# Memory attention in two token blocks, with the expert gathers of the first block beside the attention of the second

## The reference

```python
def memory_cross_attention(h, mem_n, wq, wkv, wo):      # 4 heads of 256
    q = (h @ wq).reshape(B_, S, N_XATTN_HEADS, XATTN_HEAD_DIM)
    ...
    p = jax.nn.softmax(jnp.einsum('bshd,bmhd->bhsm', q, k) * (XATTN_HEAD_DIM ** -0.5), axis=-1)
    o = jnp.einsum('bhsm,bmhd->bshd', p, v).reshape(B_, S, N_XATTN_HEADS * XATTN_HEAD_DIM)
    return o @ wo

def peer_ffn(h, wq, subkeys, u, v):                     # 8 heads, 128 x 128 experts
    q = (xt @ wq).reshape(T, PEER_HEADS, 2, PEER_HALF)
    s = jnp.einsum('thpc,hpnc->thpn', q, subkeys)
    s_top, i_top = lax.top_k(s, PEER_TOPK)              # 16 of each half
    cand = s_top[:, :, 0, :, None] + s_top[:, :, 1, None, :]
    best, pos = lax.top_k(cand.reshape(T, PEER_HEADS, 256), PEER_TOPK)
    gates = jax.nn.softmax(best, axis=-1)
    ...
    def block(args):                                    # 128 tokens at a time
        act = jax.nn.gelu(jnp.einsum('cd,ced->ce', xb, u[eb])) * gb
        return jnp.einsum('ce,ced->cd', act, v[eb])

x = x + memory_cross_attention(rms_norm(x, xattn_norm_g), rms_norm(mem, mem_norm_g), ...)
x = x + peer_ffn(rms_norm(x, ffn_norm_g), ...)
```

## Time and profile before

| what | value |
|---|---|
| median of 3 runs | 1732.67 us (1731.45 to 1732.8) |
| profiled execution | 1734.02 us, of it 1732.2 us from first to last instruction |
| mean granted clock of TensorE | 0.973 |
| busy | PE 1570.4 us (91%), DVE 1214.4 (70%), ACT 851.1 (49%), POOL 357.7 (21%) |
| 256 gathers | 312.52 to 947.35 us (issue), 268.45 MB on their queue |
| attention, from the end of `wq` to the first gather | 245 to 312.5 us |

### The profile page before, as it was taken

The page is one execution under the profiler, slowest core; times in us unless marked ns, Lnnn a source line. Parts: engine busy times, 40 slices in busy tenths (PEclk is TensorE's granted clock), DMA queues, the critical chain, the costliest instruction groups (busy, mean ns, idle before and its releaser), DMA issues.

```text
span 1732.2 us, 23839 instructions
## 1 busy us (share of the span) xinstructions
PE 1570.4 (91%) x9202; PEld 1192.7 (69%) x9202; DVE 1214.4 (70%) x2403; ACT 851.1 (49%) x1713; POOL 357.7 (21%) x326
## 2 busy tenths in 40 slices
PE   6999988789997787878888999999999999999999
PEld 5899988555542232322242688989999977789999
DVE  5797665777888888845654689666776548777764
ACT  5657734444454444433433663245554436465542
POOL 1010102344454444444433003100000200010000
PEclk9999999899999999999999999999999999899999
DMA  7333443799999999999999432024444522035544
GB/s 270 123 122 122 152 165 120 318 403 425 415 425 426 427 427 427 427 427 427 428 427 427 161 135 98 26 98 146 174 182 152 200 98 98 25 122 191 176 167 149
DMA packets 63592, 421.13 MB, mean 243 GB/s; under 512 B 8180, under 2 KB 11512, under 8 KB 15608
## 3 DMA queue, kind: packets, MB, share of 16 engines
q0 software_dynamic: 36864, 268.45, 36.9%
q1 hardware_dynamic: 23952, 148.70, 24.0%
q10 hardware_dynamic: 2664, 2.47, 0.4%
HBM read 418.54 MB, written 1.05 MB: 242 GB/s over the span
## 4 chain that ended last, share of the span: by engine, by line
PE 63%; DMA 19%; DVE 11%; ACT 5%; issue 2%; SPq 0%; ACTq 0%; DVEq 0%
PE bank L377 62%; DMA uv<-in_uv,idx 18%; DVE lows L440 3%; DVE uv L1418 2%; ACT dg L389 2%; PE bank L382 1%; DMA slabs<-in_w_in 1%; ACT wp L385 1%; ACT acts L389 1%; ACT L389 0%; DVE cacc L393 0%; ACT wf L385 0%; DVE rsb L543 0%; DVE t L722 0%; DMA slabs<-in_sk 0%
## 5 line engine op out<-in xcount | busy, mean ns | idle before, releaser
L377 PE MATMUL bank<-uv,dg 128*128 128x512 f32 x1024 | 494.6, 619 | 83.7 <-ACT dg L389 83.4
L377 PEld LDWEIGHTS bank<-uv,dg 128*128 128x128 f32 x1024 | 183.2, 193 | 373.4 <-ACT dg L389 215.3
L1418 DVE CUSTOM_DVE_ANT_0 uv<-uv,htok 128x1024 f32<-128x1024 f32 x256 | 313.0, 1223 | 163.6 <-DMA uv<-in_uv,idx 160.5
L1532 POOL DMA_INDIRECT uv<-in_uv,idx x256 | 281.4, 1099 | 372.7 <-PE bank L377 324.1
L377 PE MATMUL bank<-hn,lows 128*128 128x272 f32 (+2 forms) x704 | 200.9, 285 | 0.0
L440 DVE TENSOR_TENSOR lows<-slabs,wp 128x2048 fp32r<-128x2048 f32 (+1 forms) x78 | 167.7, 2150 | 45.9 <-ACT wp L385 45.7
L389 ACT ACTIVATE acts<-acts 128x1 f32<-128x1 f32 x256 | 51.4, 201 | 279.3 <-DVE acts L1418 278.7
L385 ACT ACTIVATE wp<-slabs 128x2048 fp32r<-128x2048 f32 (+1 forms) x78 | 140.7, 1804 | 86.1 <-DMA slabs<-in_dn 29.7
L557 POOL TENSOR_TENSOR sqT<-sqT 128x256 f32<-128x256 f32 (+1 forms) x42 | 44.4, 1058 | 623.6 <-ACT sqT L389 621.4
L440 DVE TENSOR_TENSOR lows<-slabs,whl 128x2048 fp32r<-128x2048 f32 (+1 forms) x52 | 108.2, 2081 | 36.8 <-ACT whl L385 36.7
L377 PE MATMUL bank<-hh,lows 128*128 128x272 f32 x448 | 133.1, 297 | 0.0
(11 more groups left out here) (380 smaller groups left out, 3005.0 us busy)
## 6 DMA issues: line engine op xcount, KB each, us to landing
slabs<-in_up SPq DMA_DIRECT2D x44, 1024.0 KB, 4.8
slabs<-in_w_in SPq DMA_DIRECT2D x28, 1024.0 KB, 4.8
slabs<-in_dn SPq DMA_DIRECT2D x32, 704.0 KB, 4.1
slabs<-in_wkv SPq DMA_DIRECT2D x8, 1024.0 KB, 4.8
slabs<-in_w_out SPq DMA_DIRECT2D x8, 1024.0 KB, 4.8
slabs<-in_pq SPq DMA_DIRECT2D x8, 1024.0 KB, 4.9
slabs<-in_wq SPq DMA_DIRECT2D x4, 1024.0 KB, 4.8
slabs<-in_wo SPq DMA_DIRECT2D x4, 1024.0 KB, 4.8
```

Of the source, the lines that this page charges most:

```text
L377: ins = T.e.matmul(pr[2] if len(pr) > 2 else out, pr[0], pr[1], start=(start and k == 0), stop=(stop and k == len(pairs) - 1), skip_group_ ...
L1418: V.e.tensor_tensor_reduce(u_, u_, htok[:, n, :], 1.0, 0.0, ALU.mult, ALU.add, acts[:, n, e_:e_ + 1]).then_inc(*V.up("dot", q))
L1532: G.e.indirect_dma_start(uv[q % NU][:, :], None, d["uv"][:, :], bass.IndirectOffsetOnAxis(ap=idx[:, n, e_:e_ + 1], axis=0)).then_inc(s_uv[ ...
```

## The change

The stage `xat` is gone. Its work, the end of the mixer's projection, the choice for head 0 and the gathers and accumulations up to gather 116 of the first block follow one list written out by hand (`XAT_ORDER`) that all engines walk, each taking its own tokens. Behind it the planner goes on with 2 steps for each gather.

- The attention goes by units (head, block), the first block ahead of the second. `pT` holds 128 tokens.
- The output projection is token-major: for one block, one slab and one head 6 matmuls with 256 columns (`wo.n.i.h`: block n, slab i, head h). They accumulate in banks 4 + 2n and 5 + 2n upon the residual, which is brought there by products with the identity (`xx`). The expert sums accumulate upon that in the same banks, and the final copy adds nothing.
- Of each block the gain is applied on VectorE in token-major layout (`xg`), the squares are summed by ScalarE from the bank (`sq2`), and the tokens are transposed (`ht`) and split (`hh`, `hl`). The root of the norm (`rcol`) is applied in the scores' copy and in the Gelu's scale.
- Head 0's query goes block by block (`q0`, `qe`, `qx`, `qy`, scores `s0`, their copy `sy`). Its slab (`pq.0`) has a place of its own and is loaded ahead of `wo`, as are the gains in rows (0.5 MB).
- The buffers of the gathers lie over tiles of the attention. `row_buffer_free` says what each waits for: 4, 2, 0, 1 and 3 need parts of the attention or the first block's projection, and 5, 6 and 7 need the whole output projection of the second block.

```diff
+XAT_ORDER = """
...
+xa.2.0.10 wo.0.1.1 wo.0.2.1 xa.3.0.7 xa.3.0.8 xa.1.1.1 wo.0.2.2 wo.0.1.2 lo.wo.3 xa.0.1.5 wo.0.0.1 wo.0.0.2 xa.3.0.9 xa.3.0.10
...
+wo.1.3.1 wo.1.2.3 u.4 wo.1.0.0 wo.1.0.1 wo.1.1.1 wo.1.0.2 wo.1.1.2 u.2 wo.1.0.3 wo.1.1.3 u.0 xg.1.0 u.1 wo.1.3.2
...
+            elif what == "wo":
+                _, n, i, h = x
+                k = PLACE["wo", i]
+                w = weights(k)
+                split_tensor(k)
+                T.wait_ge(*V.at("xl", h, n))
+                o = B[4 + 2 * n + i // 2][:, (i % 2) * 256:(i % 2) * 256 + 256]
+                ins = mm(o, [(O[n][q][:, c, :], w[p][:, c, :]) for c in (2 * h, 2 * h + 1) for p, q in TERMS], False, False)
...
+            elif what == "xg":
+                _, n, half = x
+                V.wait_ge(s_row, 16)
+                for i in (2 * half, 2 * half + 1):
+                    for h in range(4):
+                        V.wait_ge(*T.at("wo", n, i, h))
...
+        def row_buffer_free(q):
+
+            units = [(h, n) for h in range(4) for n in range(2)]
+            if q == 0:
+                for h in range(4):
+                    G.wait_ge(*T.at("xO", h, 0))
+            elif q in (1, 2):
+                for u in units:
+                    G.wait_ge(*T.at("xS", *u))
+            elif q == 4:
+                for u in units:
+                    G.wait_ge(*T.at("xO", *u))
+            else:
+                for i in range(4):
+                    for h in range(4):
+                        G.wait_ge(*T.at("wo", 0 if q == 3 else 1, i, h))
...
-            for q in range(2 * P + LAG):
+            begin = max(x[1] for x in done if x[0] == "u") + 1
+            for q in range(begin, 2 * P + LAG):
                 if q < 2 * P:
                     n, e_ = divmod(q, P)
                     while ("choose", n, e_ // 16, 18) not in taken:
                         pump(1, q)
                     out.append(("u", q))
-                    pump(3 if q < 16 else 2, q)
+                    pump(3 if q < 80 else 2, q)
```

More of the change, by code:

```diff
@@ L252, in build @@
         zero = top.enter_context(ExitStack())
+        with ExitStack() as ph:
+            gains = [sbuf(ph, f"row{q}", [P, NC, T1]) for q in range(2)]
         MM = [sbuf(zero, f"mm{q}", [P, NC, T1], F32R) for q in range(2)]
+        with ExitStack() as ph:
+            pq0 = sbuf(ph, "pq0", [P, 2, SLOTW], F32R)
         sc = sbuf(zero, "sc", [P, 2, 16, P])
@@ L276, in build @@
             qT = sbuf(ph, "qT", [P, 8, T1])
[L277 to L280, removed]
+            O = [[sbuf(ph, f"o0{q}", [P, NC, P], F32R) for q in range(2)]]
+            eb = [sbuf(ph, f"eb{i}", [P, T1]) for i in range(4)]
+            pT = [sbuf(ph, f"pT{i}", [P, 2, P]) for i in range(4)]
         mid.close()
@@ L288, in build @@
             oneh = sbuf(ph, "oneh", [P, 256])
-            uv = [sbuf(ph, f"uv{i}", [P, 2 * D]) for i in range(NU)]
+            with ExitStack() as two:
+                O.append([sbuf(two, f"o1{q}", [P, NC, P], F32R) for q in range(2)])
+            for i in (5, 2, 4, 1, 3, 0):
+                uv[i] = sbuf(ph, f"uv{i}", [P, 2 * D])
             dg = [sbuf(ph, f"dg{i}", [P, P]) for i in range(NDG)]
@@ L1264, in scores_of @@
             return [("spj", h, 0, 0), ("spj", h, 0, 1), ("sev", h, 0), ("spj", h, 1, 0), ("spj", h, 1, 1), ("sev", h, 1), ("ssc", h), ("scp", h)]
-        def spread(steps, more):
-            out = list(steps)
-            for k, x in enumerate(more):
-                out.insert(2 * k + 1, x)
-            return out
         def choice_of(n, h):
@@ L1276, in peer_plan @@
         def peer_plan():
-            first, second = scores_of(0), choice_of(0, 0)
-            out = first + second[:7] + [("tokens",)] + second[7:11] + [("gexp", 0, 0)] + second[11:] + scores_of(1)
-            todo = []
-            for h in range(1, 7):
-                steps = choice_of(0, h)
-                todo += [("parts", h + 1)] + spread(steps, scores_of(h + 1))
-            todo += choice_of(0, 7)
+            out, todo = [], []
+            for h in range(1, 8):
+                todo += [("parts", h)] + scores_of(h) + choice_of(0, h)
             for h in range(8):
                 todo += choice_of(1, h)
-            taken, late = {("choose", 0, 0, 18)}, []
+            done = set(XAT)
+            todo = [x for x in todo if x not in done and not (x[0] == "parts" and ("hi", "pq", x[1]) in done)]
+            taken, late = {x for x in done if x[0] == "choose" and x[3] == 18}, []
             def pump(steps, q):
@@ L1314, in build, with scores_at @@
         PEER = peer_plan()
+        def scores_at(n, h, q):
+            return sc[:, n, 2 * h + q, :] if h else sc0[:, n, q, :]
         def cand_jobs(n, h):
-            return [(sv_[:, q, :], si[:, q, :], sc[:, n, 2 * h + q, :], s2[:, q, 0:P]) for q in range(2)]
+            return [(sv_[:, q, :], si[:, q, :], scores_at(n, h, q), s2[:, q, 0:P]) for q in range(2)]
         def final_jobs():
```

761 lines of the change are left out of this document (457 added, 304 removed).

## The result

The changed kernel takes 1743.45 us (median of 7, 1737.67 to 1750.04) against 1732.8 us (median of 7, 1731.29 to 1734.88): ratio 1.0062, 95% interval 1.0048 to 1.0076. It is 10.7 us slower. I had forecast 1730; the time lies in the stated range and on the other side of no change. Its single times spread by 12 us, those of the kernel before by 4.

The account below looks back on a forecast made before the run. The gathers' transfers were taken to bound the stretch from 312.5 to 960, TensorE the rest. Head start -26.6, slabs +9.8, late indices +11.7, late buffers +2.3 sum to -2.8 us: about 1730, range 1721 to 1744.

Parts of the forecast that it names:

- Head start: Before the gathers' stream: the first gather goes at 285.9, 26.6 us earlier, with VectorE setting the start.
- the hole behind the first five: After five gathers, three wait for buffers to about 302; slabs ready by then fill the gap, charged nothing.
- Slabs: In the gathers' stream: four more slabs of 1 MB move beside gathers, adding 9.8 us.
- Late indices: At first gathers of heads 1, 3, 4 and the second block: holes for want of indices, together +11.7 us.
- L: Time of a gather from issue to landing, taken as 7.0 us between bounds 5.3 and 8.6.
- Late buffers: Beside the gathers: TensorE frees no buffers during a head's projection; one more such hole, +2.3 us.
- One more such hole, +2.3: One more head's projection beside the gathers makes TensorE free no buffers once more, as between 355 and 370 before.
- TensorE falls behind: Rival: TensorE runs out of buffers at each of six further heads, +13.8 us, 1744; chance 0.10.

Follow-up runs that it names:

- x9_four_more_before: The kernel before with one slab loaded five times instead of once in the gathers' stream, nothing waiting for it: 1741.94 us, 1.0045.
- x1_choice_early: The changed kernel with 4 instead of 2 planner steps for each gather from 117 to 127, so the second block's first indices come earlier: 1747.42 us, 1.0083.
- x8_one_product: The changed kernel with the query projections of heads 1 to 7 using the high parts alone, one product of three: 1746.32 us, 1.0081.
- x17_clumps_before: The kernel before with the second block's choices of heads 1 to 3 each laid as one clump of 19 steps, no index late: 1750.14 us, 1.01.
- x16_planner_alone: The changed kernel with its own opening and, from gather 10 on, the planner of x7_opening_planner: 1734.47 us, 1.0004.
- x15_even_steps: x7_opening_planner with 2 planner steps for a gather from gather 13 on instead of 3 up to gather 31: 1723.71 us, 0.9956.
- x7_opening_planner: The changed kernel with x3_opening's opening and, from gather 10, a planner laying the next head's score items between choice steps: 1731.68 us, 0.9995.
- x3_opening: The changed kernel with the opening alone reordered: output products and gain earlier, gathers in the order 5, 6, 7, 8, 9: 1741.82 us, 1.0058.

## Why the prediction was wrong

- **Head start: right.** 26.8 us measured, 26.6 forecast; first gather 285.69 against 285.9. The points on the way fit too: the first low part begins at 243.81 (243.7), the gain ends at 269.48 (269.6), the choice begins at 276.10 (276.0). So it isn't luck. The choice took 9.3 us, not 9.0, and from the indices to the gather it was 0.29, not 0.94. That the hole behind the first five would be covered by slabs: wrong, 8 us to gather 13. Gather 5 came at 306.05, not 302 (301.80 in another execution), and gather 9 blocked the queue. This too is a hole for want of buffers.
- **Slabs: right.** 9.8 us, and x9_four_more_before bears it out.
- **Late indices: the mechanism and about the size right.** Where the indices came last (16, 64, 128) the holes are 9.6 us; I had 11.2 for these three, since L is 5.4 to 6.3 and not 7.0. At 48 I let a slab fill the hole and had 0.5; it was 5.2 and ended on TensorE, as did the 1.5 at 80, where I had nothing; the indices were late at both as well. And to take a late index away brings little while its neighbours stay (x1_choice_early).
- **Late buffers: the step that failed.** "One more such hole, +2.3" stands against some 19 to 20 us: 8 in the opening, 5.2 and 1.5 at 48 and 80, 5 in small pieces. It priced only the case that I had read in the trace before, TensorE at a projection, and took that for the only one, though the stream before has 7.7 us of holes beside its slabs. In the changed kernel the hand-written order makes a second case: TensorE and ScalarE stand for an item of VectorE which stands behind dots of rows still on the way, or behind a clump of choice steps. The rival "TensorE falls behind" named the right waits and gave them the wrong cause. x8_one_product speaks against that cause; x17_clumps_before, x16_planner_alone, and x15_even_steps against x7_opening_planner speak for the order. I had counted places for the index writes alone, in a table, and not for the copies, and had not looked at how evenly choice steps lie between dots, though the list shows both.
- **The clock.** I left it out. The granted clock is 0.93 instead of 0.97 from 330 to 600, with windows of 5 us at 0.50, the lower of its two levels (1.2 instead of 2.4 GHz). One is 555 to 560, and TensorE stood from 550.8 to 556.6. At place 48 it had stood 6.17 us; from 434.80 to 438.5, at a granted clock of 0.53, the four matmuls of one gather take 3.7 us, where eight take 3.6 at 1.00. That is 3.7 against the 2.45 us of a gather, so such a wait costs more than itself. How much of the 10.7 us that is was not measured apart; x15_even_steps is the fastest of all at 0.95.

What stays open: the split of the holes between clumps, copies, the opening and indices in the changed kernel. They replace each other, so one-at-a-time numbers don't sum. That the order costs the time is shown by x16_planner_alone; which of its features does so in the changed kernel is argued from the places above and from x17_clumps_before and x15_even_steps, which show it in other kernels.

## What to carry to other kernels

In a stream fed by buffers, an engine in order has three duties: release (dots), feed (indices) and small answers to others (copies). Count for each of them how many rows still on the way stand ahead of it, and how long the longest piece of other work between two releases is; a piece longer than the stream can bridge can cost most of itself, though nothing in it is late (here 6.3 of 9 us). An even order by rule (two steps a gather, with the opening of x3_opening) beat one written by hand by 1.1% with the same work in it. And earliest isn't best: moving feeds ahead in one piece made it some 15 us slower. Where an instruction waits for two things, look up when each came: the engine that a view names needn't be the one that counted, and at place 48 a wait for a buffer looked like one for indices.

## What the runs showed of the hardware

A gather of 1 MB by rows lands 5.4 to 6.3 us after its issue when the stream is empty or nearly so, beside 4.8 for a slab of the same size, and takes 2.45 in a full one. With two of three products of seven projections left out, TensorE was busy 212 instead of 227 us between 330 and 600, its granted clock there fell from 0.93 to 0.89, and the kernel became no faster.
